# Four level buffers in place of three in the gated recurrence of an encoder block, and VectorE's order of the levels rearranged

## The reference, cut to what matters

```python
b = jnp.cumsum(lfb, axis=2)
diff = b[:, :, :, None, :] - b[:, :, None, :, :]
decay = jnp.exp(jnp.where(causal[None, None, :, :, None], diff, -jnp.inf))
attn = jnp.einsum('bhtk,bhtsk,bhsk->bhts', qb, decay, kb)
o = attn @ vb + jnp.einsum('bhtk,bhkv->bhtv', qb * jnp.exp(b), S)
S_new = jnp.exp(b_last[:, :, 0, :])[..., None] * S + jnp.einsum(
    'bhsk,bhsv->bhkv', kb * jnp.exp(b_last - b), vb)
```

## Time and profile before

| | us |
|---|---|
| three executions | 1116.25, 1117.04, 1118.84 (median 1117.04) |
| the profiled execution | 1116.83 |
| its span | 1115.0 |
| TensorE busy in the span | 1103.8 (99%) |
| VectorE busy | 631.6 (57%) |
| ScalarE busy | 527.8 (47%) |
| GpSimd busy | 439.2 (39%) |

### The profile page before, as it was taken

The page is one execution under the profiler, slowest core; times in us unless marked ns, Lnnn a source line. Parts: engine busy times, 40 slices in busy tenths (PEclk is TensorE's granted clock), DMA queues, the critical chain, the costliest instruction groups (busy, mean ns, idle before and its releaser), DMA issues.

```text
span 1115.0 us, 17502 instructions
## 1 busy us (share of the span) xinstructions
PE 1103.8 (99%) x6434; PEld 971.7 (87%) x6434; DVE 631.6 (57%) x923; ACT 527.8 (47%) x735; POOL 439.2 (39%) x546
## 2 busy tenths in 40 slices
PE   9999999999999999999999999999999999999997
PEld 7889999988888888888888888888899999988886
DVE  7887777442222668888668123466977777430012
ACT  6555555542323555654466443354555555542231
POOL 0000000486665544434548883163000000485651
PEclk9999999999999999999999999999999999999999
DMA  7287675332333221222313442122676665333312
GB/s 240 78 226 185 181 198 169 114 113 95 113 97 110 76 77 57 76 76 76 112 58 127 161 166 76 39 76 75 179 200 179 173 193 169 115 113 99 109 57 76
DMA packets 49458, 136.89 MB, mean 123 GB/s; under 512 B 4736, under 2 KB 11008, under 8 KB 49280
## 3 DMA queue, kind: packets, MB, share of 16 engines
q1 hardware_dynamic: 43888, 118.90, 31.2%
q0 software_dynamic: 4320, 15.73, 8.5%
q10 hardware_dynamic: 1200, 1.57, 0.4%
HBM read 134.09 MB, written 2.10 MB: 122 GB/s over the span
## 4 chain that ended last, share of the span: by engine, by line
PE 53%; POOL 25%; issue 21%; DVE 0%; POOLq 0%; DMA 0%; ACT 0%; DVEq 0%; SPq 0%; ACTq 0%
POOL wl L438 25%; PE bank L1463 8%; PE bank L1465 8%; PE bank L1464 8%; PE bank L1567 4%; PE bank L1569 4%; PE bank L1568 4%; PE score L1567 3%; PE score L1569 3%; PE score L1568 3%; PE o_bank L1567 1%; PE o_bank L1569 1%; PE o_bank L1568 1%; PE bank L1524 1%; PE bank L1528 0%
## 5 line engine op out<-in xcount | busy, mean ns | idle before, releaser
L438 POOL TENSOR_TENSOR wl<-raw,wh 128x256 fp32r<-128x256 f32 x512 | 412.9, 840 | 325.5 <-ACT wh L472 281.2
L472 ACT ACTIVATE wh<-raw 128x1024 fp32r<-128x1024 f32 x120 | 126.0, 1054 | 148.6 <-PE bank L1465 146.4
L1463 PE MATMUL bank<-xh,wh 128*128 128x512 f32 x456 | 182.3, 400 | 0.0
L1465 PE MATMUL bank<-xh,wl 128*128 128x512 f32 x456 | 177.8, 390 | 0.0
L1464 PE MATMUL bank<-xl,wh 128*128 128x512 f32 x456 | 177.5, 389 | 0.0
L452 POOL DMA_DIRECT2D raw<-w_all x30 | 26.1, 869 | 325.1 <-DMA raw<-w_all 325.1
L1463 PE MATMUL bank<-zr,wh 128*128 128x512 f32 (+1 forms) x374 | 142.5, 381 | 0.0
L1465 PE MATMUL bank<-zr,wl 128*128 128x512 f32 (+1 forms) x374 | 141.6, 379 | 0.0
L1464 PE MATMUL bank<-zr,wh 128*128 128x512 f32 (+1 forms) x374 | 140.4, 375 | 0.0
L916 DVE SCALAR_TENSOR_TENSOR x<-bank,x 128x512 f32<-128x512 f32 (+1 forms) x31 | 21.3, 686 | 175.8 <-PE bank L1465 175.8
L1464 PEld LDWEIGHTS bank<-xl,wh 128*128 128x128 f32 x456 | 85.7, 188 | 18.7 <-issue 1.7
(11 more groups left out here) (304 smaller groups left out, 2582.0 us busy)
## 6 DMA issues: line engine op xcount, KB each, us to landing
raw<-w_all SPq DMA_DIRECT2D x200, 512.0 KB, 3.3
raw<-w_all POOLq DMA_DIRECT2D x30, 512.0 KB, 5.4
zf<-w_all SPq DMA_DIRECT2D x30, 256.0 KB, 4.6
x<-x_t SPq DMA_DIRECT2D x8, 256.0 KB, 6.4
out_t<-x SPq DMA_DIRECT2D x8, 256.0 KB, 2.4
raw<-w_all SPq DMA_DIRECT2D x6, 256.0 KB, 6.2
memf<-mem_t ACTq DMA_DIRECT2D x1, 1024.0 KB, 4.8
raw<-w_all ACTq DMA_DIRECT2D x2, 256.0 KB, 4.8
```

The source lines that it names most:

```text
L438: ins = nc.gpsimd.tensor_tensor(wl[:, slot, two], raw[:, slot, two], wh[:, slot, two].bitcast(f32), SUB)
L472: nc.scalar.activation(wh[:, slot, :], raw[:, slot, :], ACT.Copy).then_inc(hi_ready, 1)
L1463: nc.tensor.matmul(out_, a[0], b_[0], start=first, stop=False)
L1465: return nc.tensor.matmul(out_, a[1], b_[0], start=False, stop=last)
```

## The change

A fourth level buffer is added, and level a uses buffer a modulo 4. `differences` for levels 4 to 6 wait for the scores of level a - 4 of the same head; for levels 0 to 3 they wait for scores of the head before (level 3 for level 3, level a for level 4 + a).

VectorE's order: `differences` 0 and 1 stand in A behind the scan for every head. L 0 has `differences` 2, 3, then `factors` 0, 1. L 1 has `factors` 2, 3, then `differences` 4, 5, then `take_scores` 0, 1. L 2 has `factors` 4, 5, `differences` 6, the difference for `kd`, `take_scores` 2, 3. K has `factors` 6, `take_scores` 4, 5 and the multiply of `kd`.

ScalarE's order: `decays` of the next pair of levels are taken one step sooner, in L a those of levels 2a + 2 and 2a + 3 (6 alone in L 2); levels 0 and 1 of heads 1 to 3 stay in L 0, ahead of 2 and 3. The exponentials of `kd` and `b` go from K to L 2. TensorE's and GpSimd's order stays.

```diff
-        X = sb("X", [128, 3, T], f32, mix_mem)
+        X = sb("X", [128, 4, T], f32, mix_mem)
...
         def x_slot(a):
-            return 2 if a == 6 else a % 2
+            return a % 4
...
             def decays(h, a):
-                for l in range(2 * a, 2 * a + 2 if a < 2 else len(LEVELS)):
+                for l in range(2 * a, min(2 * a + 2, len(LEVELS))):
...
-                if kind == "L" and (h, a) != (0, 0):
-                    decays(h, a)
-                if kind == "K":
+                if kind == "L":
+                    if (h, a) != (0, 0) and a == 0:
+                        decays(h, 0)
+                    decays(h, a + 1)
+                if kind == "L" and a == 2:
                     act.wait_ge(diff_ready, DIFFS * (h + 1))
                     nc.scalar.activation(kd[:, :], kd[:, :], ACT.Exp).then_inc(exp_ready, 1)
                     nc.scalar.activation(eb[:, :], b[:, :], ACT.Exp).then_inc(exp_ready, 1)
...
-                if a == 6 or a < 2:
-                    if h:
-                        dve.wait_ge(score_done, score_no(h - 1, 6 if a == 6 else 4 + a) + 1)
-                else:
-                    dve.wait_ge(score_done, score_no(h, a - 2) + 1)
+                if a >= 4:
+                    dve.wait_ge(score_done, score_no(h, a - 4) + 1)
+                elif h:
+                    dve.wait_ge(score_done, score_no(h - 1, 3 if a == 3 else 4 + a) + 1)
...
-                    if h == 0:
-                        differences(h, 0)
-                        differences(h, 1)
-                if kind == "L":
-                    if a == 0:
-                        dve.wait_ge(k_ready, h + 1)
-                        dve.wait_ge(silu_done, SN["q", h] + 1)
-                    if (h, a) != (0, 0):
-                        differences(h, 2 * a)
-                        differences(h, 2 * a + 1)
-                    if a == 2:
-                        differences(h, 6)
-                    if a > 0:
-                        take_scores(h, 2 * a - 2)
-                        take_scores(h, 2 * a - 1)
-                    factors(h, 2 * a)
-                    factors(h, 2 * a + 1)
-                    if a == 2:
-                        factors(h, 6)
-                if kind == "K":
+                    differences(h, 0)
+                    differences(h, 1)
+                if kind == "L" and a == 0:
+                    differences(h, 2)
+                    differences(h, 3)
+                    dve.wait_ge(k_ready, h + 1)
+                    dve.wait_ge(silu_done, SN["q", h] + 1)
+                    factors(h, 0)
+                    factors(h, 1)
+                if kind == "L" and a == 1:
+                    factors(h, 2)
+                    factors(h, 3)
+                    differences(h, 4)
+                    differences(h, 5)
+                    take_scores(h, 0)
+                    take_scores(h, 1)
+                if kind == "L" and a == 2:
+                    factors(h, 4)
+                    factors(h, 5)
+                    differences(h, 6)
                     b3 = b[:, :].rearrange("p (c t) -> p c t", t=CHUNK)
                     last = b3[:, :, CHUNK - 1:CHUNK].to_broadcast([128, NCH, CHUNK])
                     V_.tensor_tensor(kd[:, :].rearrange("p (c t) -> p c t", t=CHUNK), last, b3, SUB)\
                         .then_inc(diff_ready, 1)
+                    take_scores(h, 2)
+                    take_scores(h, 3)
+                if kind == "K":
+                    factors(h, 6)
                     take_scores(h, 4)
                     take_scores(h, 5)
```

## The result

The changed kernel takes 1134.01 us (four executions, 1127.39 to 1135.22) against 1116.67 before: 1.0139 times the time, 95% interval 1.0098 to 1.0181. The forecast was 1125.7, the range 1119.5 to 1129.0. The direction was right and the size half of it. The executions differ in TensorE's mean granted clock: 1127.39 had 0.997, the three others 0.989 to 0.991; the profiled execution of before has 0.998, and those taken beside the later runs have 0.996 to 0.999. The trace of after is that of the execution of 1134.43.

What follows compares the result with a forecast made beforehand. TensorE, busy 1103.8 of 1115.0 us, was taken as the bound. Seven waits summed to 10.9 us, less the 2.0 already there: 1116.83 + 8.9 = 1125.7, range 1119.5 to 1129.0.

Steps and rivals of the forecast that it cites:

- term 1: Head 0, first L step: four `differences` instructions beside GpSimd delay `factors`, so TensorE waits at both levels; 2.8 us.
- term 6: Head 3, levels 2 and 3: `take_scores` 0 and 1 stand behind eight level instructions; 0.3 us.
- term 2: Head 1, first scores: four `differences` instructions moved behind the scan make the first `factors` late; 1.0 us.
- term 3: Head 1, level 4: later decay and norm delay `take_scores` 2, which frees the score bank; 2.0 us.
- term 4: Head 2, level 6: ScalarE work ahead of head 1's norm delays C's eviction, then `take_scores` 4; 1.2 us.
- term 5: Head 3, first L step: `differences` 0, 1 behind the scan delay q's eviction and `factors`; 2.4 us.
- term 7: Head 3, levels 6 and 7: the norm comes later behind ScalarE's added work, with B's eviction; 1.2 us.
- Rival A: The moved work falls into VectorE's idle time and both TensorE waits go: -2.0 us, 1114.8; chance 0.04.

Runs made afterwards that it cites:

- e1: The changed kernel with eight extra TensorE matmuls ahead of the scores in each of its three longest waits: 1127.58 us.
- e3: The changed kernel with GpSimd's subtractions cut from 256 to 2 columns each: 1112.91 us.
- e4: The kernel before with four extra VectorE level instructions, results unused, ahead of head 0's first `factors`: 1123.26 us.
- e2: The kernel before with the fourth level buffer, its slots and its waits on scores, all orders as they were: 1116.52 us.
- e8: e5 without the edit that puts ScalarE's norm ahead of a slot's other steps: 1128.96 us.
- e5: The changed kernel with `factors` 0, 1 ahead of `differences` 2, 3, `take_scores` right behind `factors`, and ScalarE's norm ahead of a slot's other steps: 1114.13 us.
- e7: e5 without its first edit, so `differences` 2, 3 stay ahead of `factors` 0, 1: 1120.78 us.

## Why the prediction was wrong

The step that failed is "TensorE's busy time is unchanged, its idle time 9 more", and with it the price of a wait as its own length. TensorE's busy time rose by 9.9 us, its idle time by 7.7; the 9.9 are three falls of the granted clock, which the prediction put at nothing without naming them. The waits, in us, from the trace of after by the pitch of 0.23 (for term 1's second piece and term 6 from e1's, at full clock):

| term | forecast | measured |
|---|---|---|
| 1, head 0, both levels | 2.8 | 1.9 + 0.8 |
| 2, head 1, level 0 | 1.0 | 1.1 |
| 3, head 1, level 4 | 2.0 | 2.3 |
| 4, head 2, level 6 | 1.2 | 1.1 |
| 5, head 3, level 0 | 2.4 | 0.4 + 2.1 |
| 6, head 3, level 2 | 0.3 | 0.6 |
| 7, head 3, level 6 | 1.2 | 1.1 |
| sum | 10.9 | 11.4 |

- *Place and releaser* held: level 4 of head 1 now waits on `take_scores` (L1246), not on `factors`; level 6 of heads 2 and 3 waits where nothing waited; the norm multiply has 2 to 3 us of idle in front of it. For term 5, q's eviction comes 13.2 us later than in the earlier trace rows where TensorE is 11.7 later, 1.5 against the 1.3 I had. A part of this term lies one step earlier than I said, before the outputs (0.4, on S). Term 4's own rows give 483.7 - 482.35 = 1.3, not the 1.2 that I entered; 1.1 was measured.
- *The prices* held: four level instructions in front of head 0's `factors` at 0.88 each (e3, e4), nothing for the buffer (e2). The places are also those that the edits decide: ScalarE's order terms 3, 4 and 7 (e8 against e5), the order on VectorE terms 1 and 2 (e7 against e5). What makes the whole of term 5 isn't shown.
- *The sum* of the waits, 8.9, is therefore nearly right; by the table it is 9.4. Without a fall the change costs 9.7 by the spans of the traces and 10.8 at the median (e1).
- *The clock* is what is missing: three falls to half clock of 6.8 us in the traced execution, 9.9 us there, and 6.4 us of the median by e1. Two more executions have nearly the same mean clock (0.990, 0.991) and no trace; the fourth, 1127.39 at 0.997, lies inside the range. The trace of before gave no row of a fall: its longest wait in this stage is 1.1 us and its clock stays at full. That it never falls there isn't shown: three of 16 later executions of before have 0.996, with spans of 1116.0 to 1116.3, and no trace.
- *Rival A* (-2.0, both waits gone) fell because of its own condition, the first pair of `factors` at 377.60. With the three orders mended both waits go, and e5 measures -2.6.

Open: what decides whether the clock falls after a given wait. Full clock after 1.9 us in one execution (e7) and half clock after the same wait in others (the changed kernel, e4) is all that the runs show.

## What to carry to other kernels

Where one engine is busy 99% of the span, look for what every other engine's new order does to its few waits, in time order with the pitch of the place: here the same instruction costs VectorE 0.33 us, or 0.88 beside GpSimd's subtractions. Work that is done "a step sooner" must stand behind what the bound engine needs next, on every engine that does it, ScalarE included. And a wait of TensorE of some 2 us is to be priced with and without a fall of its clock, which here cost 3.2 us where it lasted 6.8.

## What the runs showed of the hardware

In these traces TensorE's granted clock fell from 2.4 to 1.2 GHz at or behind waits of 1.5 and 1.9 us (e4), 1.9, 2.3 and 2.1 (the changed kernel), 3.3 and 2.8 (e8). It did not fall behind those of 0.9 to 1.4 (before, the changed kernel, e7, e8), nor behind one of 1.9 (e7). A fall lasted 3.4 or 6.8 us and cost 1.6 to 1.7 or 2.9 to 3.5. Eight matmuls with no use in each of the three long waits kept the clock up and took 6.4 us off the kernel. During a fall the page still shows TensorE as busy; the mean granted clock of the execution (0.990 in place of 0.998) is the sign.

VectorE's level instructions of 128x256 start 0.33 us apart with GpSimd's subtractions cut to 2 columns (e3), and 0.88 apart beside the full ones (the changed kernel).
